# First four feature tiles of both norms turned by block moves and VectorE in a hybrid decoder block

## What is computed

```python
x = x + concat([h_m, h_g]) @ w_out                  # "OUT"
hq = rmsnorm(x, xattn_norm_g) @ wq_x                # first norm, "Q"
att = softmax(hq @ mk) @ mv
x = x + att @ wo_x                                  # "O"
hm = rmsnorm(x, mlp_norm_g) @ w1                    # second norm, MLP
x = x + square(relu(hm)) @ w2
```

## Time and profile before

| what | value |
|---|---|
| runs | 2820.93, 2829.07, 2831.23 us; median 2829.07 |
| profiled execution, from its first to its last instruction | 2824.3 us |
| PE busy, share of the span | 99% |
| DVE, ACT, POOL busy | 64%, 54%, 37% |
| mean granted clock of PE | 0.998 |
| HBM | 134 GB/s over the span |

### The profile page before, as it was taken

One profiled execution on the slowest core, in us unless ns is written; L12 is line 12 of the kernel. 1 busy time (PEld: TensorE's weight loads), 2 busy tenths in 40 slices (PEclk: granted clock), 3 DMA queues, 4 the chain that ended last, 5 costly groups with the idle time before them and its releaser, 6 DMA issues.

```text
span 2824.3 us, 44962 instructions
## 1 busy us (share of the span) xinstructions
PE 2800.3 (99%) x15076; PEld 2330.9 (83%) x15076; DVE 1812.8 (64%) x3011; ACT 1514.2 (54%) x3126; POOL 1057.3 (37%) x1334
## 2 busy tenths in 40 slices
PE   8999999999999999999999999999999999999998
PEld 8888888788878888888888888888888888888887
DVE  6376774766686755457687674466668675545665
ACT  6554444556555444556565554465655644455553
POOL 5264574644345500234546320044435550023440
PEclk9999999999999999999999999999999999999999
DMA  6732586555552222355654222255556222234442
GB/s 217 249 105 68 175 292 235 186 173 147 150 196 83 73 93 90 100 177 153 175 164 145 74 83 90 90 157 169 144 150 201 83 73 93 90 102 144 150 149 82
DMA packets 185906, 393.41 MB, mean 139 GB/s; under 512 B 14224, under 2 KB 14368, under 8 KB 185664
## 3 DMA queue, kind: packets, MB, share of 16 engines
q1 hardware_dynamic: 160112, 309.89, 35.8%
q0 software_dynamic: 22880, 75.72, 8.0%
q10 hardware_dynamic: 2672, 4.76, 0.4%
HBM read 346.24 MB, written 33.59 MB: 134 GB/s over the span
## 4 chain that ended last, share of the span: by engine, by line
PE 97%; DVE 1%; issue 1%; DMA 1%; ACT 0%; DVEq 0%; POOL 0%; ACTq 0%
PE bank L1975 44%; PE work L1975 22%; PE bank L2342 17%; PE work L2342 3%; PE work L1989 1%; PE bank L2380 1%; PE work L2091 1%; PE bank L1989 1%; PE work L2129 1%; PE work L2037 1%; PE work L2151 1%; PE work L2240 1%; PE work L2244 1%; PE work L2239 1%; PE work L2223 1%
## 5 line engine op out<-in xcount | busy, mean ns | idle before, releaser
L899 ACT ACTIVATE w_hi<-raw 128x512 fp32r<-128x512 f32 x1156 | 724.7, 630 | 1018.9 <-PE bank L1975 515.8
L1413 DVE TENSOR_TENSOR w_lo<-raw,w_hi 128x512 fp32r<-128x512 f32 x657 | 475.8, 728 | 792.9 <-ACT w_hi L899 791.4
L1411 DVE SCALAR_TENSOR_TENSOR w_lo<-raw,w_hi 128x512 fp32r<-128x512 f32 x499 | 448.1, 918 | 95.3 <-ACT w_hi L899 94.1
L734 POOL TENSOR_TENSOR hr<-qk 128x256 f32<-128x256 f32 x60 | 44.3, 738 | 790.0 <-ACT qk L1287 790.0
L2342 PE MATMUL bank<-w_hi,h_hi 128*128 128x512 f32 x720 | 280.3, 389 | 0.1
L2342 PE MATMUL bank<-w_lo,h_hi 128*128 128x512 f32 x720 | 280.1, 389 | 0.0
L2342 PE MATMUL bank<-w_hi,h_lo 128*128 128x512 f32 x720 | 280.1, 389 | 0.0
L1975 PE MATMUL bank<-w_hi,x_hi 128*128 128x512 f32 x640 | 255.2, 399 | 0.0
L1975 PE MATMUL bank<-w_lo,x_hi 128*128 128x512 f32 x640 | 249.6, 390 | 0.0
L1975 PE MATMUL bank<-w_hi,x_lo 128*128 128x512 f32 x640 | 249.4, 390 | 0.0
L724 POOL TENSOR_TENSOR h_lo<-qk,h_hi 128x256 fp32r<-128x256 f32 x180 | 188.0, 1064 | 67.2 <-ACT h_hi L1300 67.2
(11 more groups left out here) (399 smaller groups left out, 6473.6 us busy)
## 6 DMA issues: line engine op xcount, KB each, us to landing
raw<-in_w_dram SPq DMA_DIRECT2D x226, 512.0 KB, 3.9
raw<-sums_dram SPq DMA_DIRECT2D x120, 512.0 KB, 3.8
raw<-in_w_in_dram SPq DMA_DIRECT2D x112, 512.0 KB, 3.6
raw<-in_w_out_dram SPq DMA_DIRECT2D x32, 512.0 KB, 4.1
raw<-kq_dram SPq DMA_DIRECT2D x32, 512.0 KB, 3.7
raw<-vo_dram SPq DMA_DIRECT2D x32, 512.0 KB, 3.7
xres<-in_x_dram POOLq DMA_DIRECT2D x16, 512.0 KB, 6.1
early_rows<-in_w_dram POOLq DMA_DIRECT2D x8, 1024.0 KB, 9.1
```

Of the source, the lines that this page charges most:

```text
L734: nc.gpsimd.tensor_tensor(diff[:, kt, :], quarter(0, 0, kt), quarter(0, 1, kt), ALU.subtract).then_inc(diff_ready, 1)
L899: nc.scalar.activation(w_hi[:, slot, :], raw[:, pair_slot, slot % 2, :], ACT.Copy).then_inc(slab_hi, 1)
L1411: ins = stt(out=w_lo[:, slot, :], in0=src, scalar=1.0, in1=hi, op0=ALU.mult, op1=ALU.subtract)
L1413: ins = tt(w_lo[:, slot, :], src, hi, ALU.subtract)
```

## The change

Tiles 0 to 3 of both norms are no longer turned by PE. ACT issues 16 DMAs of 64 KB in step KT + 1 of OUT and of O (`move_rows`); each moves 32x32 blocks of the first half of `xres` into the upper half of `qk` (runs of 32 numbers, 128 bytes, as the existing moves on POOL's queue have them). In step KT + 5 DVE waits for all 16 and turns the blocks by four 128x512 transposes into the lower half of `qk` (`turn_rows`). ACT's high halves and DVE's low halves are made from there, in steps KT + 6 and KT + 7 instead of KT + 2 and KT + 3, and in a step that has both they now stand ahead of `add_block`. `xres` is kept as two halves of columns, so that a half is contiguous over the four row tiles; loads, stores, squares and adds follow. Tiles 4 to 7 are turned by PE as before.

```diff
-TURNS = 28
+TURNS = 20
-TURN_EARLY = {KT + 2: (0, 1, 2, 3)}
-DRAIN_EARLY = {KT + 2: (0, 1), KT + 3: (2, 3)}
+MOVE_ROWS, TURN_ROWS = KT + 1, KT + 5
+DRAIN_EARLY = {KT + 6: (0, 1), KT + 7: (2, 3)}
...
-        xres = sb("xres", [P, NCH, D])
+        xres = sb("xres", [P, 2, NCH, COLS])
+        res_blocks = qk[:, HEADS:, :]
+        res_turned = qk[:, 0:HEADS, :]
...
+                def move_rows(k):
+                    act.wait_ge(bank_free, use_no(g, (U_OUT, U_O)[k] + 4))
+                    for q in range(4):
+                        for a in range(4):
+                            dst = res_blocks[32 * q:32 * q + 32].rearrange("p c (k a j) -> p (c k) a j", a=4, j=32)[:, :, a, :]
+                            src = xres[32 * a:32 * a + 32, 0].rearrange("p c (k q j) -> p (c k) q j", q=4, j=32)[:, :, q, :]
+                            act.dma_start(dst, src).then_inc(rows_in, 16)
...
+                    if kt < HALF:
+                        act.wait_ge(rows_turned, 2 * HALF * g + HALF * k + kt + 1)
+                        nc.scalar.activation(into[:, kt, :], res_turned[:, kt, :], ACT.Copy,
+                                             scale=norm_g[:, k + 1, kt:kt + 1]).then_inc(act_hi_ready, 1)
...
                 for s in range(B_OUT * KT, B_Q * KT):
                     split(g, s)
                     mix_tiles(s)
+                    if s == B_OUT * KT + MOVE_ROWS:
+                        move_rows(0)
...
+                def turn_rows(k):
+                    dve.wait_ge(rows_in, 16 * 16 * (2 * g + k + 1))
+                    for kt in range(HALF):
+                        nc.vector.transpose(out=res_turned[:, kt, :].rearrange("p (c n) -> p c n", c=NCH),
+                                            in_=res_blocks[:, :, kt * P:(kt + 1) * P]).then_inc(rows_turned, 1)
...
+                    if s == B_OUT * KT + TURN_ROWS:
+                        turn_rows(0)
+                    for kt in DRAIN_EARLY.get(s - B_OUT * KT, ()):
+                        norm_tile(0, kt, (h_hi, h_lo))
                     if s % KT == KT - 1:
                         b = s // KT - B_OUT
                         dve.wait_ge(x_in, 16 * NCH * (g + 1))
-                        add_block(U_OUT + 4 * b, b * COLS, (wbank, bank)[b])
-                    for kt in DRAIN_EARLY.get(s - B_OUT * KT, ()):
-                        norm_tile(0, kt, (h_hi, h_lo))
+                        add_block(U_OUT + 4 * b, b, (wbank, bank)[b])
...
-                    for kt in TURN_EARLY.get(s - B_OUT * KT, ()):
-                        norm_tile(0, kt, U_OUT)
...
-                    for kt in TURN_EARLY.get(r, ()):
-                        norm_tile(1, kt, U_O)
```

More of the change, by code:

```diff
@@ L452, in sums_done, with halves @@
             eng.wait_ge(sums_stored[n % 4], 16 * (n // 4 + 1))
+        def halves(rows):
+            return rows.rearrange("p (h n) -> p h n", h=2)
         def per_pass(g, n, hb, k):
@@ L633, in _ @@
             for i in range(NCH):
-                pool.dma_start(xres[:, i, :], A["x"][i * P:(i + 1) * P, :]).then_inc(x_in, 16)
+                pool.dma_start(xres[:, :, i, :], halves(A["x"][i * P:(i + 1) * P, :])).then_inc(x_in, 16)
             tmp = qk[:, 0, 0:P]
@@ L869, in group @@
                     stand_alone(pool)
-                    pool.dma_start(out[bass.ds(g * GROUP + i * P, P), :], xres[:, i, :]).then_inc(stored, 16)
+                    pool.dma_start(halves(out[bass.ds(g * GROUP + i * P, P), :]), xres[:, :, i, :]).then_inc(stored, 16)
                 pool.wait_ge(stored, 16 * NCH * (g + 1))
@@ L939, in tile_hi, with sum_squares @@
                 ins.then_inc(act_hi_ready, 1)
-            def sum_squares(i, src=xres, squares=tok):
-                nc.scalar.activation(squares[:, i, :], src[:, i, :], ACT.Square,
-                                     accum_out=ss[:, i:i + 1]).then_inc(norm_ss, 1)
+            def sum_squares(i, src=None, squares=tok):
+                if src is None:
+                    ins = nc.scalar.activation(halves(squares[:, i, :]), xres[:, :, i, :], ACT.Square,
+                                               accum_out=ss[:, i:i + 1])
+                else:
+                    ins = nc.scalar.activation(squares[:, i, :], src[:, i, :], ACT.Square, accum_out=ss[:, i:i + 1])
+                ins.then_inc(norm_ss, 1)
             def guess(n, count):
@@ L1085, in sum_half @@
                     here = slice(half * COLS, (half + 1) * COLS)
-                    nc.scalar.activation(tok[:, i, here], xres[:, i, here], ACT.Square,
+                    nc.scalar.activation(tok[:, i, here], xres[:, half, i, :], ACT.Square,
                                          accum_out=(ss, ss_b)[half][:, i:i + 1]).then_inc(half_ss, 1)
@@ L1476, in _ @@
                 if KT + 5 <= s < KT + 5 + NCH:
[L1477 removed]
+                    scale_x(s - KT - 5)
                 for kt in DRAIN_X.get(s, ()):
@@ L1544, in norm_step, with add_block @@
                             link(tt(rs_mlp[:], rs_mlp[:], rs_mlp[:], ALU.mult))
-                def add_block(u, col, out_of=bank):
+                def add_block(u, half, out_of=bank):
                     for i in range(4):
                         full(u + i)
-                        v = xres[:, i, col:col + COLS]
+                        v = xres[:, half, i, :]
                         tt(v, out_of[i][:], v, ALU.add).then_inc(bank_free, 1)
@@ L1565, in final_row @@
                 def final_row(i):
-                    stt(out=xres[:, i, :], in0=xres[:, i, :], scalar=rstd[:, i:i + 1], in1=fin_g[:], op0=ALU.mult,
+                    stt(out=xres[:, :, i, :], in0=xres[:, :, i, :], scalar=rstd[:, i:i + 1], in1=halves(fin_g[:]), op0=ALU.mult,
                         op1=ALU.mult).then_inc(tok_ready, 1)
@@ L1979, in slab, with tiles_out @@
                     ins.then_inc(slab_used, 1)
-            def tiles_out(count0, ready, src_rows, tiles=range(KT), src=tok, into=wbank):
+            def tiles_out(count0, ready, src_rows, tiles=range(KT), src=tok, into=wbank, col=0):
                 for kt in tiles:
```

49 lines of the change are left out of this document (31 added, 18 removed).

## The result

The changed kernel took 2864.11 us (median, 2860.27 to 2865.42), the kernel before 2826.85 us (2820.93 to 2831.23) beside it: 1.0128 times, 95% interval 1.0116 to 1.0140, so 37 us slower. I had forecast 2841.5. The profiled execution of after took 2864.93 us, 1.5 more than its span; what I had put as 4.8 us between span and median of the kernel before is this 1.5 and scatter.

A forecast was written before the change was run, and what follows sets the result against it. PE was taken to bound the kernel (97% of the chain). Terms -14.0 + 5.6 + 3 + 18 + 3.8 - 4 = +12.4 us on the 2824.3 us span gave 2836.7, 2841.5 on the median; range 2816 to 2900.

The forecast's parts named there:

- ACT's issues: 16 DMAs behind ACT's split in OUT: 384 ns each, 6.1 us, hidden within 8.9 us; bounds gave stalls of 1.5 and 2.8.
- The rival that has ACT held by its own issues: ACT free only when moves land; weights' split stalls 1.5 to 2.8 us in groups 1 to 3; 2848 to 2856; chance 0.10.
- The landing: DVE's wait for the moves: late by 0 to 2.7 us, taken as 0.5 for six moves of groups 1 to 3, 3 us.
- Group 0: Moves share DMA engines with POOL's 1 MB transfers: late by 14 us in OUT (0 to 35), 4 in O (0 to 10).
- the clock: After each of group 0's two stalls PE runs mostly at 1.2 GHz for a while: 3.8 us together.
- my -4 us for a smaller backlog: In group 0 a later PE finds less backlog of POOL and DVE: -4 us, between 0 and -8.
- the high halves' move from PSUM to SBUF: High halves read from SBUF instead of PSUM hide beside the same work: priced at nothing.
- the 1.0 us that I took for the order: End of OUT, two low halves ahead of the adds: PE late by 1.0 us once a group, bounds 0 and 1.4.
- The orders: DVE's order delays PE 1.0 us at OUT's end and 0.4 in O, in four groups: 5.6 us.
- The transposes: 128 transposes fewer on PE, in 8 batches of 16 at 1.75 us: 14.0 us off the chain.

The follow-up runs named there:

- the other forms of the moves: Changed kernel with half of each move's runs left out in OUT, and 128 runs of 512 bytes per move in O: 2846.26 us.
- the run with both pauses: Changed kernel with moves split between SyncE and ACT, turned in step 12, POOL pausing in group 0 after sums 1 and 10 until moves land: 2818.75 us, ratio 0.9997.

## Why the prediction was wrong

**The failed step** is "ACT's issues", where I took 384 ns for each DMA from ACT's load of 512 runs. An issue of this kind takes 651 ns, so 16 take 10.9 us and not 6.1, and the "hidden" became a stall of 1.5 to 1.7 us in six places, 9.7 us in all. My bound of 652 ns and "a stall of 1.5 us" from POOL's row was the measured one; I had preferred a row with the same queue and count of runs over one with the same kind of copy, and the other forms of the moves showed that the count of runs has nothing to do with it. The rival that has ACT held by its own issues was right about the place, in all eight, and its 1.5 to 2.8 us for groups 1 to 3 hold; it had a chance of 0.10. Its reason, a queue that takes a DMA only when earlier ones have drained, fits group 0 alone: elsewhere the issues went at a fixed 0.65 us, and POOL's at 0.65 us never stretched.

**The landing**: taken as 3 us in groups 1 to 3, measured 0. The last lands 2.1 us after its issue. The 10 to 18 ns for a run were right, 48.4% of 13 us over 528 packets for each engine is 12 ns, but runs are hidden beneath the pace of the issues.

**Group 0** was taken as 18 us for the landings, 1.4 for the orders and 3.8 for the clock. Measured waits: 14.0 for `w_lo` and 4.8 for the adds in OUT, 6.1 and 1.4 in O, 26.3 in all. The cause, packets beside POOL's transfers, was right, and the 14 us in OUT to the digit, by luck: I had them on DVE waiting for a landing, and they were on ACT, whose issues stretched to 22.4 us beside this traffic. The rule that I weighed, the Trainium skill, "DMA: Bandwidth & Descriptors", section "Queues, rings and completion order", that an engine takes turns packet by packet, agrees in direction with the window of 347 to 360 us, but not one for one: 3186 packets of q10 passed beside 950 of the other two queues. Taken strictly it gave 30 us or more for the runs and up to 35 of lateness; the burst of issues took 22.4 and PE waited 14.0. The low clock cost some 5.5 us: half of PE's busy time in four stretches at 1.2 GHz, less the two that before has. With the transposes' -3.5 us and the 2.1 us of the earlier trace rows gone, 26.3 + 5.5 - 3.5 - 2.1 = 26.2, and group 0 grew by 26.4. Of my -4 us for a smaller backlog nothing showed but these 2.1.

**A term that I didn't have**: the low halves' source. I priced the high halves' move from PSUM to SBUF at nothing, rightly, and didn't ask the same of DVE's. In group 0 a pair took 2.1 us too much in OUT and 1.0 in O of after, and two pairs 4.9 us in the run with both pauses. In OUT of after the chain that ended last runs through them: two low halves of h in 3.47 us and two of weights in 1.55 and 1.74 us, 4.0 us above their prices, stand ahead of the add for which PE waits 4.8 us, where the other groups wait 0.7 to 0.8.

```profile
379.52 1.55 DVE L1444 TENSOR_TENSOR w_lo<-raw,w_hi 128x512 fp32r<-128x512 f32 x1
380.99 3.47 DVE L1556 SCALAR_TENSOR_TENSOR h_lo<-qk,norm_g,h_hi 128x512 fp32r<-128x512 f32 x2
384.38 1.74 DVE L1444 TENSOR_TENSOR w_lo<-raw,w_hi 128x512 fp32r<-128x512 f32 x1
```

So the 1.0 us that I took for the order holds without this term only. The Trainium skill says it in "SBUF — State Buffer", section "SBUF: two separate sides": DVE and GpSimd share a pair of ports under an exclusive lock, which a DVE instruction with two SBUF inputs needs against a GpSimd one that reads SBUF. The runs agree: up to 4.21 us a pair beside POOL's additions and 1.41 without them.

**The orders**: 5.6 us taken, 4.1 measured for OUT's part by the two runs without DMAs, where I had 4.0 for it. In O the wait for `act_lo` was 0.2 us in groups 1 to 3, against 0.4.

**The transposes**: -3.5 us a group was right in groups 1 to 3 (the run without DMAs and adds first), nothing was left of it in group 0.

**The sum.** DVE's first addition of the MLP stands 2.0 us later in group 1 of after than before, counted from the group's start: -3.5 + 5.5 (the waits name 4.0 of the 5.5). Three such are 6, group 0 is 26.4, the start 1.0. The other 5.7 of the 39.1 us lie behind the turned tiles, most in group 1: 0.45 us in each of its four MLP passes and 2.9 at its end. Of these, 1.3 are a longer wait that the profile names "issue" of PE itself, the rest are transposes behind it at the lower clock. Such a wait was also 1.6 us in group 0 of before, and 1.7 in group 1 of the run without DMAs. I have no run that ties the 5.7 to the change, and leave them open.

Against the forecast's +12.4 on the span, 26.7 us are missing. Group 0 has 10.7 of them (26.4 against 18 + 3.8 - 4 + 1.4 - 3.5 = 15.7), groups 1 to 3 have 15.0 (11.7 against 3 + 4.2 - 10.5 = -3.3), the start 1.0. In groups 1 to 3, ACT's issues are 6.7 of the 15.0: 9.7 of waits where 3 had been taken for the landing.

## What to carry to other kernels

A row of DMAs is work of the engine that issues it: count issues times the time of the nearest issue of the same kind (here 0.65 us for a copy inside SBUF, not 0.38 as for a load), and put it against that engine's slack. Splitting it over two queues, with the turn moved forward, made the change level here; spreading it in time made it worse. When an operand moves from PSUM to SBUF, look who else uses SBUF at that time, and read the rows of an operation of that engine that has both operands there already. A pass of 14 us taken off the bounding engine is worth its price only where its replacement meets no other traffic; look at the one group that is not like the others.

## What was not expected of the hardware

- Issues of ACT and SyncE stretch beside POOL's 1 MB transfers: single ones took up to 3.54 us on ACT and 4.41 on SyncE in group 0, at most 0.71 and 1.51 in the other groups of the same runs, while POOL's took 0.65 to 0.68 in the same traffic. That they wait for earlier ones to drain is my reading; no view shows it.
- Two engines issuing at once took 6.7 and 6.6 us for eight each in OUT of group 1 (at the 0.68 us from start to start of the burst it would be 5.4), so the parallel issue costs a fifth more there; in O of the same group it was 6.3 and 5.9.
- Spreading the same 16 issues over four steps made the last landing later, 4.79 us after issue instead of 2.1, and the kernel some 25 us slower than with the burst (1.0215 against 1.0128 of the kernel before).
- The time of an issue with the queues otherwise free doesn't depend on the number of runs, from 128 to 512.
- An operation of DVE with both operands in SBUF was slowed beside POOL's (0.67 to 1.26 us in group 1), one with an operand in PSUM was not (0.74).
